# A recurrent layer's gate products: three reduced-precision products of split operands in place of one float32 product

## The reference, cut to what matters

```python
def lru_coeffs(xc, gw, gb, lam):
    xb = xc.reshape(B_, L, LRU_BLOCKS, LRU_BLOCK)
    gates = jax.nn.sigmoid(jnp.einsum("blnc,gncd->gblnd", xb, gw) + gb[:, None, None])
    r, i = gates[0], gates[1]
    log_a = -LRU_C * r * jax.nn.softplus(-lam)
    a = jnp.exp(log_a)
    b = jnp.sqrt(-jnp.expm1(2.0 * log_a)) * (i * xc)
    return a, b
...
u, g = jnp.split(h @ w_in, 2, axis=-1)      # latent and context alike
xc = dwconv(u, conv_w, conv_b)              # 4 taps along the tokens
# for both directions: h_t = a_t * h_(t-1) + b_t, context first, then latent
y = ((forward + backward) * jax.nn.silu(g)) @ w_out
```

## Time and profile before

| what | value |
|---|---|
| median of 3 runs | 2505.1 us (2501.42 to 2505.3) |
| the profiled execution, own time | 2505.53 us |
| its span | 2503.7 us |
| busy PE / DVE / ACT / POOL | 2477.3 / 1477.3 / 1179.9 / 265.5 us |
| mean granted clock of TensorE | 0.998 of full |
| the recurrent layer, first to last gate products | from 1206.4 us of the span |

### The profile page before, as it was taken

How to read it: one execution, slowest core, us unless ns; L and a number is a source line. 1 busy time by engine, 2 the same in 40 slices (tenths; PEclk the granted TensorE clock), 3 DMA queues, 4 the chain that set the end, 5 groups by cost and what they waited for, 6 DMA issues and landing times.

```text
span 2503.7 us, 31491 instructions
## 1 busy us (share of the span) xinstructions
PE 2477.3 (99%) x11984; PEld 1943.5 (78%) x11984; DVE 1477.3 (59%) x1951; ACT 1179.9 (47%) x1742; POOL 265.5 (11%) x140
## 2 busy tenths in 40 slices
PE   7999999999999999999999999999999999999999
PEld 6887777777777677788877777788887887877877
DVE  5644444554545554566776767734746576665775
ACT  5644344553444434456656565624525335243463
POOL 0000000000000000002555555100400000000000
PEclk9999999999999999999999999999999999999999
DMA  7568777736787777765333333324435444344434
GB/s 259 174 200 266 248 252 253 245 102 224 246 266 250 240 254 255 244 236 164 93 97 92 95 93 92 118 84 135 143 102 159 127 126 143 117 148 131 127 108 151
DMA packets 278131, 429.43 MB, mean 172 GB/s; under 512 B 14566, under 2 KB 93180, under 8 KB 277116
## 3 DMA queue, kind: packets, MB, share of 16 engines
q1 hardware_dynamic: 277260, 422.54, 52.9%
q10 hardware_dynamic: 752, 5.26, 0.5%
HBM read 425.64 MB, written 2.10 MB: 171 GB/s over the span
## 4 chain that ended last, share of the span: by engine, by line
PE 95%; DMA 1%; ACT 1%; DVE 1%; issue 1%; SPq 0%; DVEq 0%; ACTq 0%
PE ps L778 66%; PE ps L1170 13%; PE ps L851 3%; PE ps L1153 2%; PE ps L960 1%; PE ps L1281 1%; PE ps L933 1%; PE ps L1299 1%; PE ps L829 1%; PE ps L1125 1%; PE ps L862 1%; DMA ring<-in_ev_w_mem_kv 1%; PE ps L945 1%; DMA ring<-in_att_w_in 0%; PE ps L1290 0%
## 5 line engine op out<-in xcount | busy, mean ns | idle before, releaser
L1423 ACT CAST ring_hi<-ring 128x1024 fp32r<-128x1024 f32 (+2 forms) x598 | 619.8, 1039 | 953.9 <-PE ps L778 533.2
L1950 DVE TENSOR_TENSOR ring_lo<-ring,ring_hi 128x1024 fp32r<-128x1024 f32 (+2 forms) x520 | 626.4, 1210 | 632.0 <-ACT ring_hi L1423 629.6
L778 PE MATMUL ps<-ring_hi,act_hi 128*128 128x512 f32 (+2 forms) x1272 | 514.1, 404 | 6.4 <-DVE vectors_t L2177 4.3
L778 PE MATMUL ps<-ring_hi,act_lo 128*128 128x512 f32 (+2 forms) x1272 | 493.0, 388 | 0.0
L778 PE MATMUL ps<-ring_lo,act_hi 128*128 128x512 f32 (+2 forms) x1272 | 491.6, 386 | 0.0
L778 PE MATMUL ps<-ring_hi,features_hi 128*128 128x512 f32 x1152 | 457.7, 397 | 1.1 <-ACT second_block L1740 0.9
L778 PE MATMUL ps<-ring_hi,features_lo 128*128 128x512 f32 x1152 | 449.3, 390 | 0.0
L778 PE MATMUL ps<-ring_lo,features_hi 128*128 128x512 f32 x1152 | 448.6, 389 | 0.0
L778 PEld LDWEIGHTS ps<-ring_hi,act_hi 128*128 128x128 f32 x1272 | 240.2, 189 | 109.3 <-issue 41.4
L778 PEld LDWEIGHTS ps<-ring_hi,act_lo 128*128 128x128 f32 x1272 | 239.9, 189 | 51.1
L778 PEld LDWEIGHTS ps<-ring_lo,act_hi 128*128 128x128 f32 x1272 | 240.7, 189 | 41.9
(11 more groups left out here) (277 smaller groups left out, 2453.4 us busy)
## 6 DMA issues: line engine op xcount, KB each, us to landing
ring<-in_mod_w SPq DMA_DIRECT2D x192, 512.0 KB, 4.9
ring<-in_att_w_in SPq DMA_DIRECT2D x128, 512.0 KB, 3.8
ring<-in_ev_w_in SPq DMA_DIRECT2D x104, 512.0 KB, 4.6
ring<-in_od_w_in SPq DMA_DIRECT2D x96, 512.0 KB, 4.5
ring<-in_lru_w_in SPq DMA_DIRECT2D x64, 512.0 KB, 4.1
ring<-in_ev_w_out SPq DMA_DIRECT2D x40, 512.0 KB, 4.7
ring<-in_lru_w_out SPq DMA_DIRECT2D x40, 512.0 KB, 3.6
ring<-in_od_w_out SPq DMA_DIRECT2D x36, 512.0 KB, 3.9
```

The costliest lines, as they stand in the source:

```text
L778: mm = pe.matmul(PS[:, bank, 0:n], a, w[:, k - k0, :], start=(k == k_first and j == 0), stop=(k == k_last and j == 2))
L1423: act.copy(high(U, n), raw(U, n)).then_inc(s_hi, 1)
L1950: dve.tensor_tensor(out=low(U, n), in0=raw(U, n), in1=high(U, n).bitcast(F32), op=ALU.subtract).then_inc(s_lo, 1)
```

## The change

The four float32 gate products of a block become twelve float32r products. For that the gate weights and the convolved rows are split, each by one more cast and one more subtraction a block:

- DVE casts the gate weights of the next block and subtracts (`gate_weights`), ahead of `decays`. The low part is written over the weights themselves. The high part has one buffer, so DVE waits until the gates of the block before are done. For block 0 this stands ahead of the first `conv`.
- ACT casts the convolved rows (`conv_hi`) ahead of its last cast of a ring unit, once `conv` is done.
- POOL subtracts (`conv_lo`) between its second and third ring_lo subtraction.
- PE waits for both low parts.

The new tiles (conv_hi, conv_lo, gate_weights_hi, 512 columns each) lie in space that the layer does not use. In the last block, DVE waits for the last gates before it reuses that space.

```diff
             def lru_gates(b, i=None):
                 n = lambda plus: at(b + plus, i, 2)
-                pe.wait_ge(s_xc, n(3))
-                pe.wait_ge(s_gw[b], at(64, i, 64))
+                pe.wait_ge(s_xcl, n(1))
+                pe.wait_ge(s_gwl, n(1))
                 pe.wait_ge(s_sg, n(1))
                 for j in range(4):
-                    mm = pe.matmul(PS[:, 4 + j, :], GW[:, b, j, :], XC[:, b, :, :].rearrange("p c s -> p (c s)"),
-                                   start=True, stop=True)
+                    gh, gl = GWH[:, j * P:(j + 1) * P], GWL[:, b, j, :]
+                    for part, (w, x) in enumerate(((gh, XCH), (gl, XCH), (gh, XCL))):
+                        mm = pe.matmul(PS[:, 4 + j, :], w, x, start=(part == 0), stop=(part == 2))
                 mm.then_inc(s_gt, 1)
...
-            his("lru_in", range(4, 8))
+            his("lru_in", range(4, 7))
+            act.wait_ge(s_xc, 3)
+            act.copy(XCH, XC[:, 0, :, :].rearrange("p c s -> p (c s)")).then_inc(s_xch, 1)
+            his("lru_in", [7])
             act.sem_inc(s_sg, 1)
...
+            def conv_hi(b, i=None):
+                act.wait_ge(s_xc, at(b + 3, i, 2))
+                act.copy(XCH, XC[:, b % 2, :, :].rearrange("p c s -> p (c s)")).then_inc(s_xch, 1)
...
                 for u in range(early, 4):
+                    if u == 3:
+                        conv_hi(b + 1, i)
                     hi(ahead + u, UNIT, i, 8)
...
+            def gate_weights(n, b, landed, before=True):
+
+                dve.wait_ge(s_gw[b], landed)
+                if before:
+                    dve.wait_ge(s_gt, n(0))
+                gw = GW[:, b, :, :].rearrange("p j d -> p (j d)")
+                dve.tensor_copy(GWH, gw).then_inc(s_gwh, 1)
+                dve.wait_ge(s_gwh, n(1))
+                dve.tensor_tensor(out=GWL[:, b, :, :].rearrange("p j d -> p (j d)"), in0=gw, in1=GWH.bitcast(F32), op=ALU.subtract).then_inc(s_gwl, 1)
...
+            gate_weights(block_n(0), 0, 64, False)
             conv(block_n(0), 0)
...
                 for b in range(2):
+                    gate_weights(block_n(b + 1, i), 1 - b, at(64 * (b + 1), i, 64))
                     decays(block_n(b, i), b)
                     conv(block_n(b + 1, i), 1 - b)
                     recur(block_n(b, i))
+            gate_weights(block_n(KT - 1), 1, 64 * KT // 2)
             decays(block_n(KT - 2), 0)
...
+            def conv_lo(b, i=None):
+                pool.wait_ge(s_xch, at(b + 1, i, 2))
+                pool.tensor_tensor(out=XCL, in0=XC[:, b % 2, :, :].rearrange("p c s -> p (c s)"), in1=XCH.bitcast(F32), op=ALU.subtract).then_inc(s_xcl, 1)
...
             for b in range(2):
                 for u in range(4):
+                    if (b, u) == (1, 2):
+                        conv_lo(0)
                     weights_lo(UNIT0["lru_in"] + 4 * b + u)
             with pool.Fori(0, KT // 2 - 1) as i:
                 for b in range(2):
                     lru_ix(b, i)
                     for u in range(4):
+                        if u == 2:
+                            conv_lo(b + 1, i)
                         weights_lo(UNIT0["lru_in"] + 4 * b + 8 + u, i)
```

More of the change, by code:

```diff
@@ L466, in build @@
             CSTA = sb("consts_first", [P, NCONST - NCONST_ALL], owner=first)
+        with ExitStack() as recurrent:
+            sb("second_block_first", [P, 9216], owner=recurrent)
+            GWLB = sb("gate_weights_lo", [P, 1024], F32R, owner=recurrent)
+            sb("second_block_mid", [P, 15872 - 10240], owner=recurrent)
+            XCH = sb("conv_hi", [P, 512], F32R, owner=recurrent)[:]
+            XCL = sb("conv_lo", [P, 512], F32R, owner=recurrent)[:]
+            GWH = sb("gate_weights_hi", [P, 512], F32R, owner=recurrent)[:]
         BUF = sb("second_block", [P, 17536])
@@ L539, in build @@
         LTMP = l_hs
+        GWL = GWLB[:].rearrange("p (b j d) -> p b j d", b=2, j=4)
         LA = LAF.rearrange("p (d s) -> p d s", d=2)
@@ L599, in build @@
         s_gw = [sem(f"gate_weights_landed{b}") for b in range(2)]
+        s_xch, s_xcl, s_gwh, s_gwl = map(sem, ("conv_rows_hi", "conv_rows_lo", "gate_weights_hi", "gate_weights_lo"))
         s_ri = sem("last_gates_taken")
@@ L2430, in _ @@
             y_lo(2, 6, FTH, FTL, YL, 0)
+            dve.wait_ge(s_gt, KT)
             for j in range(2):
@@ L2787, in _ @@
                 weights_lo(UNIT0["lru_out"] + u)
+            conv_lo(KT - 1)
             lru_ix(KT - 1)
```

## The result

The changed kernel takes 2526.27 us (median of 4 runs, 2525.83 to 2527.33) against 2505.2 us before: a ratio of 1.0091, 95% interval [1.0078, 1.0104], slower by 21 us. The forecast was 2528.

What follows compares the result with a forecast made beforehand. The prediction took a DVE-ACT ring (25.26 us), as long as PE's period (25.21), as the bound. Looped cycles 18.2, fifteenth 1.2, start 3.9, end -0.4 gave +22.9 on 2505.5: 2528.4 us; 8-in-10 range 2514 to 2535.

Steps and rivals of the forecast that it cites:

- the ring: Recurrent layer's loop y, sigmoids, decays, convolution, scan, y, without a wait on PE: 25.26 us a cycle, PE's period 25.21.
- The weight split on DVE at 0: Cast and subtraction of gate weights, 1.0 us a block, fit DVE's 6.86 us wait for tanh: cost 0.
- The cast on ACT at 0: Casting the convolved rows, 0.6 us, after the third cast of weights on ACT: cost 0.
- `conv_lo` at 1.3 us a cycle: POOL's subtraction of convolved rows lies on the ring: +1.3 us a cycle, bounds 0 and 1.5, 18.2 over 14 cycles.
- The replay in the prediction: Turn-by-turn account of one loop cycle from y: POOL and DVE alternate, conv_lo ends at 18.2, ring becomes 26.6 us.
- the fifteenth: Cycle after the fourteen looped ones, POOL nearly free: conv_lo still falls between L2381 and the scans, 1.2 us.
- The start at 3.9 us: Start of the layer: weights' cast ahead of the first convolution makes first sigmoids 3.9 us later, bounds 0 and 5.
- a fall of the clock in the new pauses: PE's granted clock falling in the new pauses would make the total wrong; no size or chance given.
- The end at -0.4 us: Output projection's start after the last y: low parts of the first rows set it, 1.8 us after y: -0.4 us.
- PE's saving coming through: Rival: holds leave the ring, which falls below 25.2, so PE's -0.72 x 16 = -11.5 us counts: 2494; 8%.
- The ring stays: Rival: conv_lo slips in without holding DVE, ring 25.26, start partly paid: 0 to +4, 2505 to 2509; 6%.
- The cover of the weight split: Rival that it fails: the split's cast and subtraction land on the ring, +1.0 x 15 more, 2543; 5%.

Runs made afterwards that it cites:

- e1: The changed kernel with one float32 product a gate again, on the high parts alone, all splits kept; 2525.8 us.
- e7: The kernel before (float32 gates) with low parts of each block's third and fourth ring unit made by DVE at the cycle's start, not POOL; 2502.9 us.
- e5: The changed kernel with low parts of each block's third and fourth ring unit made by DVE at the cycle's start, not POOL; 2501.6 us.
- e6: The changed kernel with the edits of e5 and e3 together; 2497.2 us, ratio to the kernel before 0.9972.
- e9: e6 with the first block's conv_lo subtraction on DVE, ahead of its product over the residual rows, not on POOL; 2493.6 us.
- e2: The changed kernel without POOL's conv_lo subtraction, the third gate product taking the high rows again; 2509.3 us.
- e3: The changed kernel with the first block's weight split behind the first convolution, not ahead of it; 2520.3 us.
- e4: The changed kernel with POOL's conv_lo subtraction done twice in a row; 2541.6 us.
- e8: The changed kernel with the conv_lo subtraction on DVE, between the recurrence's first product and the scans, not on POOL; 2519.9 us.

## Why the prediction was right, point by point

- **What bounds the stage.** Right. In the changed kernel the ring of ACT and DVE set the pace, not PE. e1 puts PE's 0.72 us a block back and nothing moves. e7 shortens the ring of the kernel before alone and nothing moves either, since there the two were equally long. PE stands 1.48 us before each gate group, where 2 were forecast.
- **The weight split on DVE at 0.** Right for the loop: two rows of 0.42 and 0.69 us inside DVE's wait.
- **The cast on ACT at 0.** Right: it lies ahead of a wait of 3.5 us for the gates.
- **`conv_lo` at 1.3 us a cycle.** Right in kind, too big in size. It measured 1.00: 13 cycles from 1217.06 to 1558.55 are 26.27 us each, and 25.27 before. The replay in the prediction had `conv_lo` end at 18.2 (18.1 in the trace) and y at 26.6 (26.25). The surplus lies in the turns behind it, where the scans and the two long subtractions got 0.4 us more than their rows took. The fourteen looped cycles cost 14.0 us and not 18.2; the fifteenth 0.95 us (1.2 forecast).
- **The start at 3.9 us.** Too small: 6.5 us, outside the bounds of 0 and 5. DVE, POOL, PE and ACT ahead of the first cycle of the changed kernel:

```profile
1198.47 2.48 DVE L2394 CAST gate_weights_hi<-second_block 128x512 fp32r<-128x512 f32 x1
...
1200.99 2.79 DVE L2396 TENSOR_TENSOR gate_weights_lo<-second_block,gate_weights_hi 128x512 fp32r<-128x512 f32 x1
...
1203.70 0.80 DVE L2381 TENSOR_SCALAR second_block<-ps,scalars 128x512 f32<-128x512 f32 x1
...
1207.58 2.65 POOL L2800 TENSOR_TENSOR conv_lo<-second_block,conv_hi 128x512 fp32r<-128x512 f32 x1 [4.35 <-ACT conv_hi L1714]
...
1210.33 0.76 PE L1164 MATMUL ps<-conv_hi,gate_weights_hi 128*128 128x512 f32 x1 [5.14 <-POOL conv_lo L2800]
...
1211.74 0.63 PE L1164 MATMUL ps<-conv_hi,gate_weights_hi 128*128 128x512 f32 x1
...
1212.17 0.63 PE L1164 MATMUL ps<-conv_hi,gate_weights_lo 128*128 128x512 f32 x1
...
1215.49 0.40 PE L1180 MATMUL ps<-features_hi,ring_hi 128*128 128x512 f32 x1
...
1217.06 2.42 ACT L1733 ACTIVATE second_block<-ps,scalars 128x512 f32<-128x512 f32 x4
```

This execution entered the layer 0.98 us earlier than that of the earlier trace rows: the held cast starts at 1167.96 and not at 1168.94. With that added, the weight split (1198.47 to 1203.78) delays the convolution by 4.2 us (4.4 forecast), and the gates start at 1211.3, as forecast. But the first twelve products were priced at 0.227 us each; they ran 0.43 us apart until the next block's products, 2.4 us more. That is the term that was missing. (The 2.2 us for a 2048-column row are 2.3 by the prediction's own figures; the sum does not feel it.) The columns of the next view are the stretch, then busy time of PE, PEld, DVE, ACT and POOL, PE's granted clock, and the DMA share:

```profile
core 0: us, PE busy (x) PEld busy (x) DVE busy (x) ACT busy (x) POOL busy (x), PEclk, DMA share, GB/s
...
1210.50:1215.00 4.50, 4.50 (x11) 3.53 (x12) 1.87 (x1) 0.00 (x0) 4.50 (x2) 0.50 0.00 0
...
1216.00:1221.00 5.00, 5.00 (x24) 4.14 (x23) 1.92 (x2) 4.97 (x7) 1.89 (x2) 1.00 0.18 52
```

PE had stood for 5.14 us before. The granted clock is then 0.50, which is the 1.2 GHz level, and 1.00 again in the block that follows. The prediction had named a fall of the clock in the new pauses as a way for the total to be wrong, but gave it no price. In the loop's pauses of 1.5 us the clock stayed at its upper level, here it did not. The sigmoids show 1217.06 - 1211.52 = 5.5, and 6.5 with the earlier entry.

- **The end at -0.4 us.** Right. The last y's and the projection's start:

```profile
1584.08 0.69 DVE L2423 TENSOR_TENSOR second_block<-second_block 128x512 f32 x1
...
1606.68 0.69 DVE L2423 TENSOR_TENSOR second_block<-second_block 128x512 f32<-128x512 f32 x1
...
1609.25 0.47 PE L787 MATMUL ps<-ring_hi,features_hi 128*128 128x512 f32 x1 [1.12 <-DVE features_lo L2429]
```

PE starts 1.9 us after y (1607.37), released by the low rows; forecast 1.8.

- **The sum.** 6.5 + 14.0 + 0.95 - 0.4 = 21.05, less the 0.98 of the earlier entry 20.1; the spans differ by 20.3 (2503.7 and 2524.0). The forecast's 22.9 had one term 2.6 us too small and another 4.2 us too big. They partly cancelled, so that the total came closer than its parts is luck.
- **The rivals.** PE's saving coming through was wrong for this kernel, but its point of decision was right: once the ring is below PE's block (e5, e6) the cycle falls to PE's 24.48, and with the start mended as well (e6, e9) the total falls too. "The ring stays" would have been 2505 to 2509; e2 gives about that (2509.3), by leaving `conv_lo` out. The cover of the weight split did not fail.

`conv_lo` is about 1.2 us of POOL work, and it costs 0.8 to 1.0 us of ring wherever it was added or taken away. The Trainium skill states in "SBUF — State Buffer", section "SBUF: two separate sides", that GpSimd and a VectorE instruction with two SBUF inputs exclude each other for whole instructions. This case's rows agree: with `conv_lo` added the scans' row grew from 4.67 to 7.64 us, and the convolution, which reads PSUM, took 2.32 us beside POOL's subtraction at 1414.49, where the earlier trace rows has 2.31. The price is most of POOL's own time, not all of it; why a part of it does not show was not settled.

## What to carry to other kernels

A saving on the busiest engine counts only if the loop that paces the stage goes through it: compare the periods of both, and look at which of two waits ends last before the instruction that needs both. Work that is moved to GpSimd is not free for VectorE, so place it where VectorE waits or reads PSUM, and count most of its length for each turn (here 0.8 to 1.0 us for 1.2). When a stage is balanced to a few hundredths of a microsecond between two rings, shorten both or neither: here the shorter ring alone gave nothing (e7), the shorter gates alone lost 21 us, and both together, with two edits at the start of the stage, gained 10 (e9; without those two edits, 2 us that are not clear of noise, e5).

## What the runs showed of the hardware

A pause of 5.1 us ahead of the first gates was followed by 5.2 us of products at the lower of TensorE's two clocks (0.43 us apart, granted 0.50). In e3 a pause of 2.37 us at the same place was followed by four products 0.23 to 0.30 us apart and then by slow ones (granted 0.58 from 1208 to 1212). In e6 a pause of the same 2.37 us was followed by slow products from the first. Ahead of the changed kernel's last gates stood a pause of 2.04 us, and most of those twelve products were 0.43 us apart again. PE's next product waited for DVE's low rows after that, so it cost nothing.

The changed kernel's looped cycles had a pause of 1.5 us in every 26 and kept the clock at 1.00. In e4 the pauses were 2.4 us: in the cycles from 1269.70 to 1432.72 the gate products stayed 0.23 us apart, but at 1459.90, 1514.24 and 1568.56, after pauses of the same length, they ran 0.43 us apart from the first. So the length of the pause alone does not decide what follows it. These runs do not show what does.

The 1170 us ahead of the layer, which are the same program in all these kernels, took up to 5 us more or less from one execution to another: the held cast of the earlier trace rows starts at 1164.64 us in e8 and at 1169.71 in e4. A start inside the layer can be compared between two traces only after that difference is taken off.
